# Tokens 512 to 767 of a product-key expert layer: all expert rows streamed through TensorE in place of gathered rows

## The reference, cut to what matters

```
q = (xt @ w_q).reshape(t, PEER_HEADS, 2, PEER_HALF)
s = einsum('thkc,knc->thkn', q, sub_keys)
top_s, top_i = top_k(s, 16)                    # per side, then 16 of the 256 sums
expert_idx, gate = ..., softmax(best_s)
h   = einsum('td,thkd->thk', xb, expert_u[ib])
act = gelu(h) * gb
out = einsum('thk,thkd->td', act, expert_v[ib])
h = layer_norm(DN_ALPHA * h + out)
```

## Time and profile before

| what | value |
|---|---|
| median of 3 runs | 3679.25 us (3676.4 to 3683.01) |
| profiled execution: span from first to last instruction | 3675.9 us |
| mean granted clock of PE | 0.852 |
| busy: PE, DVE, ACT, POOL | 78%, 73%, 28%, 56% of the span |
| moved by DMA | 1394.94 MB, 379 GB/s over the span |

### The profile page before, as it was taken

The page is one execution under the profiler, slowest core; times in us unless marked ns, Lnnn a source line. Parts: engine busy times, 40 slices in busy tenths (PEclk is TensorE's granted clock), DMA queues, the critical chain, the costliest instruction groups (busy, mean ns, idle before and its releaser), DMA issues.

```text
span 3675.9 us, 46161 instructions
## 1 busy us (share of the span) xinstructions
PE 2884.2 (78%) x16052; PEld 2038.9 (55%) x16052; DVE 2685.9 (73%) x5763; ACT 1040.2 (28%) x2694; POOL 2061.1 (56%) x1839
## 2 busy tenths in 40 slices
PE   8984988889889889999988869999977853443443
PEld 7884877578778436877775427878764410000000
DVE  3318874989874798778676887778776886667667
ACT  5511542234331213444412114444312110001000
POOL 0004543556554677777666676777656676555552
PEclk9997999899899889999999879999988866555555
DMA  6568998999888999999999999999999999999997
GB/s 245 211 226 317 395 410 355 399 376 358 323 336 332 411 410 402 393 406 409 388 411 411 410 393 410 408 400 393 410 392 407 396 405 413 421 421 421 421 420 313
DMA packets 316566, 1394.94 MB, mean 379 GB/s; under 512 B 35376, under 2 KB 40880, under 8 KB 251824
## 3 DMA queue, kind: packets, MB, share of 16 engines
q0 software_dynamic: 262656, 1073.86, 73.5%
q1 hardware_dynamic: 52384, 313.42, 21.5%
q10 hardware_dynamic: 1296, 4.72, 0.3%
HBM read 1387.66 MB, written 4.19 MB: 379 GB/s over the span
## 4 chain that ended last, share of the span: by engine, by line
PE 36%; DMA 27%; issue 14%; POOL 11%; DVE 9%; ACT 2%; DVEq 1%; SPq 0%; ACTq 0%; POOLq 0%
PE main L639 16%; DMA rowbuf<-ev,idx 9%; POOL rowbuf L596 8%; DMA rowbuf<-euv,idx 5%; PE main L647 4%; PE vbank L727 4%; PE main L838 3%; PE main L853 3%; DMA ring<-euv,idx 3%; DMA rowbuf<-eu,idx 2%; DVE rowbuf L1646 2%; DVE acc L1672 2%; PE turn L710 2%; DMA merged<-euv,idx 2%; DMA xT<-euv,idx 2%
## 5 line engine op out<-in xcount | busy, mean ns | idle before, releaser
L596 POOL DMA_INDIRECT rowbuf<-eu,idx x714 | 835.5, 1170 | 849.2 <-DVE hdot L1646 328.4
L596 POOL DMA_INDIRECT rowbuf<-ev,idx x713 | 767.3, 1076 | 370.6 <-issue 192.3
L1646 DVE CUSTOM_DVE_ANT_0 rowbuf<-rowbuf,hb 128x1024 f32<-128x1024 f32 x620 | 757.8, 1223 | 154.4 <-DMA rowbuf<-eu,idx 86.9
L639 PE MATMUL main<-xT,ring 128*128 128x256 f32 (+1 forms) x4480 | 804.6, 340 | 50.5 <-ACT mm L1109 39.8
L639 PEld LDWEIGHTS main<-xT,ring 128*128 128x128 f32 x4480 | 719.4, 193 | 138.5 <-issue 69.0
L727 PE MATMUL vbank<-rowbuf,vdiag 64*64 64x512 f32 x3008 | 512.3, 778 | 256.6 <-DMA rowbuf<-ev,idx 134.5
L1672 DVE SCALAR_TENSOR_TENSOR acc<-rowbuf,hact,acc 128x1024 f32<-128x1024 f32 x421 | 541.7, 1287 | 95.2 <-DMA rowbuf<-ev,idx 86.2
L727 PEld LDWEIGHTS vbank<-rowbuf,vdiag 64*64 64x64 f32 x3008 | 106.2, 158 | 581.2 <-ACT vdiag L1058 323.0
L1058 ACT ACTIVATE vdiag<-spots,hact 128x64 f32<-128x64 f32 x536 | 169.0, 343 | 553.6 <-DVE hact L1655 348.4
L838 PE MATMUL main<-late,ring 128*128 128x256 f32 (+1 forms) x1280 | 236.5, 348 | 36.7 <-issue 26.1
L1646 DVE CUSTOM_DVE_ANT_0 rowbuf<-rowbuf,hbank 128x1024 f32<-128x1024 f32 x178 | 215.8, 1216 | 47.1 <-DMA rowbuf<-eu,idx 39.1
(11 more groups left out here) (250 smaller groups left out, 3902.7 us busy)
## 6 DMA issues: line engine op xcount, KB each, us to landing
ring<-wblocks SPq DMA_DIRECT2D x280, 1024.0 KB, 8.2
rowbuf<-eu,idx POOLq DMA_INDIRECT x714, 12.6
rowbuf<-ev,idx POOLq DMA_INDIRECT x713, 13.1
pw<-poolw SPq DMA_DIRECT2D x20, 256.0 KB
h_out<-acc ACTq DMA_DIRECT2D x8, 512.0 KB, 7.5
xT<-xt SPq DMA_DIRECT2D x3, 1024.0 KB, 13.2
zy<-x SPq DMA_DIRECT2D x3, 1024.0 KB, 12.9
craw_ln<-ln1g SPq DMA_DIRECT2D x5, 512.0 KB, 14.5
```

The costliest lines, as they stand in the source:

```text
L596: pool.indirect_dma_start(rows[r], None, (eu, ev)[table], bass.IndirectOffsetOnAxis(ap=idx[c % 2][:, u, k:k + 1], axis=0)).then_inc(row_re ...
L639: last = pe.matmul(dst_[:, ct * tc:(ct + 1) * tc], w[:, k, ct * P:(ct + 1) * P], src[:, k, 0:tc], start=(k == 0), stop=(k == KD - 1))
L1646: last = dve.tensor_tensor_reduce(r, r, h, 1.0, 0.0, ALU.mult, ALU.add, hdot[:, g % 2, k:k + 1])
```

## The change: what it does

Superchunk 3 (`DENSE`, tokens 512 to 767, tiles 4 and 5) gathers no rows. Its picks leave the order of steps, which shrinks from 1024 to 768. In their place:

1. **Table of gates.** After the picks of superchunk 3 are known, they are split into row and column number of the 128 x 128 experts (`split_picks`) and transposed (`transposed_picks`). For each of the 256 tokens a product of two one-hot matrices (one with the gates as its values) gives a 128 x 128 matrix that holds the token's gate at each expert (`spread_gates`; `hot_rows` on DVE and `hot_columns` on ACT make the one-hot rows). 64 jobs of four tokens each do this at steps 489 to 531, around the end of superchunk 4's front; ACT evicts each job and stores the table in DRAM (`evict_job`, 16 stores of 1 MB).
2. **Experts.** 128 blocks of 1 MB (`dblocks`), each with U and V of 128 experts, come through the ring. PE scores a block for 256 tokens (`score_experts`), ACT takes the gelu (`gelu_experts`), DVE multiplies by a slice of the table (`weigh_experts`; slices for 8 blocks each are loaded by `load_slice` in pieces of 512 bytes), and PE adds the product with V into four banks (`sum_experts`, two blocks behind the score). The blocks are spread over steps 534 to 762.
3. **Around it.** `WIDTHS` gives superchunks 1 to 4 70, 140, 140 and 140 steps, so the front's last step is 513; `PAIRED` is 544. All convolutions are done on DVE (`FILL = NC`). There are 9 row buffers for 12, none of the ring's among the pair buffers (11 for 16), `LEAD2` is 4 for 7 and `GROUP` 2 for 4. Three sets of hidden rows, picks and gates are held for two (`HELD`). PE sums no row from step 534 on.

```diff
+DENSE = 3
...
-ROWS = 12
+ROWS = 9
...
-PAIRED = 800
-GROUP = 4
-LEAD2 = 7
+PAIRED = 544
+GROUP = 2
+LEAD2 = 4
-PAIRS = TILES * TILE
-WIDTHS = ((128, 28, 16, 42, 24), (40, 6, 6, 12, 12), (88, 16, 10, 34, 32), (124, 26, 16, 40, 38), (128, 28, 16, 42, 42))
+GATHERED = [t for t in range(TILES) if not FIRST[DENSE] <= t < FIRST[DENSE + 1]]
+GTILES = len(GATHERED)
+PAIRS = GTILES * TILE
+HELD = 3
+WIDTHS = ((128, 28, 16, 42, 24), (40, 8, 6, 8, 8), (81, 21, 12, 13, 13), (81, 21, 12, 13, 13), (81, 21, 12, 13, 13))
...
+FILL = NC
+
+
+SPREAD = 16
+QUAD = 4
+QUADS = NT * P // QUAD
+HOT = 4
+JOBS = 2 + QUADS + 4
+SPLIT_AT = BEGIN[NC - 1] + sum(WIDTHS[NC - 1][:2]) + 3
+JOB_BEGIN, JOB_END = BEGIN[NC - 1] + sum(WIDTHS[NC - 1][:3]) + 1, END + 18
+JOB_AT = [SPLIT_AT + 1] * 2 + [JOB_BEGIN + j * (JOB_END - JOB_BEGIN) // (JOBS - 2) for j in range(JOBS - 2)]
+DENSE_BEGIN, DENSE_END = JOB_END + 2, PAIRS - 6
+DENSE_AT = [DENSE_BEGIN + i * (DENSE_END - DENSE_BEGIN) // KEYS for i in range(KEYS)]
+SLICE = 8
+SLICES = KEYS // SLICE
+
+
...
+SHARES = ((0.0, 0.0, 0.0, 0.0), (0.2, 0.7, 1.0, 1.0), (0.1, 0.7, 1.0, 1.0), (0.1, 0.7, 1.0, 1.0), (0.1, 0.7, 1.0, 0.8))
...
+        both = [late[:, 0:2 * D], late[:, 2 * D:4 * D], early[:, :], merged[:, :, :].rearrange("p k t -> p (k t)"),
+                hb[(DENSE - 1) % HELD][:, :, :].rearrange("p t d -> p (t d)"), zy[:, :], mmscr[:, 0:2 * D]]
+        SPACES = len(both)
+        both += [rowbuf[:, r * D:(r + 2) * D] for r in range(0, ROWS - 1, 2)]
         BOTHS = len(both)
...
+            def load_slice(n):
+                sp.dma_start(slices[n % 2], spreadg[:, :, ds(n * SLICE * SPREAD, SLICE * SPREAD)].rearrange("g p n -> p g n")
+                             ).then_inc(slice_ready[n % 2], 16)
+
+            def load_expert(i):
+                r = i % RING
+                sp.wait_ge(block_done, NC * BLOCKS + i + 1)
+                sp.dma_start(ring[r][:, :, :], dblocks[ds(i, 1), :, :].rearrange("o p (k n) -> (o p) k n", k=KD)
+                             ).then_inc(w_ready[r], 16)
+
...
+            for i in range(RING):
+                load_expert(i)
+            for b in range(2):
+                sp.wait_ge(staged[b], 16 * SPREAD // 2)
+            for n in range(2):
+                load_slice(n)
+            for i in range(RING, KEYS):
+                load_expert(i)
+                n = i // SLICE + 1
+                if i % SLICE == 5 and 2 <= n < SLICES:
+                    sp.wait_ge(dense_weighed, (n - 1) * SLICE)
+                    load_slice(n)
...
+            def spread_gates(j):
+
+                g = j - 2
+                dst_ = job_bank(j)
+                pe.wait_ge(hot_row_ready, g + 1)
+                pe.wait_ge(hot_act_ready, g + 1)
+                for n in range(QUAD):
+                    last = pe.matmul(dst_[:, n * P:(n + 1) * P], hot_col[g % HOT][:, n, :], hot_row[g % HOT][:, n, :],
+                                     start=True, stop=True)
+                last.then_inc(job_made, 1)
+
+            def turned_hidden(j):
...
+            def score_experts(i):
+
+                if i == 0:
+                    pe.wait_ge(main_free, MAIN_AT[NC][0] + BANKS)
+                    pe.wait_ge(turn_free, TURN_AT[NC][0] + BANKS)
+                    pe.wait_ge(job_free, JOBS)
+                if i >= 2:
+                    pe.wait_ge(dense_gelu, i - 1)
+                pe.wait_ge(w_ready[i % RING], (NC * (BLOCKS // RING) + i // RING + 1) * 16)
+                w = ring[i % RING][:, 0:4, :].rearrange("p a (b n) -> p (a b) n", b=2)
+                dst_ = main[i % 2][:, 0:T]
+                for k in range(KD):
+                    last = pe.matmul(dst_, w[:, k, :], hTd[k // 4][:, k % 4, :], start=(k == 0), stop=(k == KD - 1))
+                last.then_inc(dense_scored, 1)
+
+            def sum_experts(i):
+
+                pe.wait_ge(dense_weighed, i + 1)
+                w = ring[i % RING][:, 4:8, :].rearrange("p a n -> p (a n)")
+                for n in range(NT):
+                    for half in range(2):
+                        last = pe.matmul(dsum[n][half], dact[i % 2][:, n * P:(n + 1) * P], w[:, half * 512:(half + 1) * 512],
+                                         start=(i == 0), stop=(i == KEYS - 1), skip_group_check=True)
+                last.then_inc(block_done, 1)
+
+            def experts(i):
+
+                score_experts(i)
+                if i >= 2:
+                    sum_experts(i - 2)
+                if i == KEYS - 1:
+                    sum_experts(i - 1)
+                    sum_experts(i)
+                    pe.wait_ge(block_done, NC * BLOCKS + RING + KEYS)
+                    pe.sem_inc(dense_done, 1)
+
+            at = now = 0
 
             def until(p):
...
+            def hot_columns(g):
+
+                if g == 0:
+                    act.wait_ge(pair_merged, NC * 4)
+                    act.wait_ge(job_free, 2)
+                if g >= HOT:
+                    act.wait_ge(job_made, 2 + g - HOT + 1)
+                for n in range(QUAD // 2):
+                    act.activation(hot_col[g % HOT][:, n, :], numbers[:, :], ACT.Square, scale=-1.0,
+                                   bias=colT[:, g * QUAD + n:g * QUAD + n + 1])
+                act.drain()
+                for n in range(QUAD // 2):
+                    t = slice(g * QUAD + n, g * QUAD + n + 1)
+                    last = act.activation(hot_col[g % HOT][:, n, :], hot_col[g % HOT][:, n, :], ACT.Relu, scale=minusT[:, t],
+                                          bias=gateT[:, t])
+                last.then_inc(hot_act_ready, 1)
+
+            def evict_job(j):
...
+            def evict_job(j):
+
+                act.wait_ge(job_made, j + 1)
+                src = hbank[:, (j % 2) * 512:(j % 2 + 1) * 512]
+                if j == 0:
+                    act.copy(rowT, src[:, 0:T])
+                    act.copy(colT, src[:, T:2 * T]).then_inc(job_free, 1)
+                elif j == 1:
+                    act.copy(gateT, src[:, 0:T])
+                    act.activation(minusT, src[:, 0:T], ACT.Copy, scale=-1.0).then_inc(job_free, 1)
+                elif j < 2 + QUADS:
+                    m, n = divmod(j - 2, SPREAD // QUAD)
+                    if n == 0:
+                        if m == 0:
+                            act.wait_ge(st_used, 2 * AJ * TILES + STATE)
+                        if m >= 2:
+                            act.wait_ge(staged[m % 2], 16 * (m // 2))
+                    to = staging[m % 2].rearrange("p (i t) -> p t i", t=SPREAD)[:, n * QUAD:(n + 1) * QUAD, :]
+                    act.copy(to, src.rearrange("p (t i) -> p t i", t=QUAD)).then_inc(job_free, 1)
+                    if n == SPREAD // QUAD - 1:
+                        act.wait_ge(job_free, j + 1)
+                        act.dma_start(spreadg[m, :, :], staging[m % 2]).then_inc(staged[m % 2], 16)
+                else:
+                    n, half = divmod(j - 2 - QUADS, 2)
+                    if n == 0:
+                        act.wait_ge(h_ready, TILES)
...
+            def gelu_experts(i):
+
+                act.wait_ge(dense_scored, i + 1)
+                if i >= 2:
+                    act.wait_ge(dense_weighed, i - 1)
+                act.activation(dgel[i % 2], main[i % 2][:, 0:T], ACT.Gelu
+                               ).then_inc(dense_gelu, 1)
...
+            def hot_rows(g):
+
+                if g == 0:
+                    dve.wait_ge(job_free, 2)
+                if g >= HOT:
+                    dve.wait_ge(job_made, 2 + g - HOT + 1)
+                t = slice(g * QUAD, (g + 1) * QUAD)
+                for n in range(QUAD // 2, QUAD):
+                    at_ = slice(g * QUAD + n, g * QUAD + n + 1)
+                    dve.tensor_scalar(hot_col[g % HOT][:, n, :], numbers[:, :], colT[:, at_], gateT[:, at_], ALU.is_equal, ALU.mult)
+                dve.tensor_tensor(hot_row[g % HOT], numbers[:, :].unsqueeze(1).to_broadcast([P, QUAD, KEYS]),
+                                  spread(rowT[:, t], KEYS), ALU.is_equal).then_inc(hot_row_ready, 1)
+
+            def weigh_experts(i):
+
+                n, m = divmod(i, SLICE)
+                dve.wait_ge(dense_gelu, i + 1)
+                if m == 0:
+                    dve.wait_ge(slice_ready[n % 2], 16 * (n // 2 + 1))
+                if i >= 2:
+                    dve.wait_ge(block_done, NC * BLOCKS + RING + i - 1)
+                dve.tensor_tensor(dact[i % 2].rearrange("p (g t) -> p g t", g=SPREAD),
+                                  dgel[i % 2].rearrange("p (g t) -> p g t", g=SPREAD),
+                                  slices[n % 2][:, :, m * SPREAD:(m + 1) * SPREAD], ALU.mult).then_inc(dense_weighed, 1)
+
+            def finish_dense(n):
+
```

More of the change, by code:

```diff
@@ L102, with at_step @@
 CONV = (0, 1, 3, 4)
-FILL = 3
+FILL = NC
[11 more added lines that the diff above has]
+SLICES = KEYS // SLICE
+def at_step(table, p):
+    return [n for n, q in enumerate(table) if q == p]
 def made_main(c, m):
@@ L196, in spans_of_bank @@
     found = []
```

(39 more changed lines are left out.)

271 lines of the change are left out of this document (162 added, 109 removed).

## The result

The changed kernel takes **3919.3 us** (median of 5 runs, 3916.23 to 3938.69) against 3679.25 us before: a ratio of 1.066, 95% interval 1.063 to 1.068. The sign of the forecast (3783 us, slower) was right, its size was not: 240 us were added where 104 had been forecast. The profiled execution has a span of 3937.0 us; it is the slowest of the five, 19 us above the execution that gives the median, so some 19 us of what follows belong to it alone.

The account below looks back on a forecast made before the run. Before, PE and DVE bound the front, with transfers close behind, and transfers alone the tail. Front 2688, tail 1072 and end 20 gave 3780 us, 3783 on the runs' scale, 2.8% slower; range 3570 to 3960.

Parts of the forecast that it names:

- front, to the first expert's score: Superchunks 1 to 4 and the table of gates, priced mainly by DVE's work: experts begin at 2688 us.
- PE's instructions, 128 experts: Tail: each expert block takes PE 7.07 us at full clock, 905 us for 128.
- start, and other stalls on DVE: Tail start: two slices must land before the first sum, 25 us (10 to 46).
- waits for blocks and slices: Tail: PE waits 72 us for late block landings and 70 us for blocks queued behind slices.
- clock and the rest: Tail: PE taken at full clock, 2.4 GHz, so nothing was added.
- after the last sum: End of kernel: evictions, norm and store, two dense tiles one behind the other, 20 us.
- The rival that dealt with it: Tail: stalls in each expert keep PE at 1.2 GHz, 905 us more, near 4690; chance 0.03.
- The ring: Tail: a block is freed only by its sum, leaving one expert's time for the next load; 72 us (0 to 322).
- the formula: Tail: with landing time L, each expert waits (L - 7.07)/2; 0.56 us taken, times 128.
- The slices' 70 us: Tail: fourteen 1 MB slices in 512-byte pieces delay the block behind them, 5 us each (0 to 238 in all).
- The slices' rival at 3951: Tail: slices served in turn with backlogged gathers land in 38 us, stalling 17 us each, 238 for 70; chance 0.19.
- The faster rival: PE sets the front, stage A 25 us shorter each; tail at transfers' pace, 966 us; 3602 us; chance 0.30.

Follow-up runs that it names:

- layout: Changed kernel with the gate table laid out by slices in DRAM, so a slice is read in 8 KB pieces: 3864.5 us.
- halves: Changed kernel with each expert block loaded as two 0.5 MB loads, U reloaded after its score, V after its sum: 3802.2 us, ratio 1.033.
- halves, slices on ACT: Changed kernel with each expert block loaded as two 0.5 MB loads and slices 2 to 15 issued on ACT's own queue: 3779.7 us.
- all three cures: Changed kernel with two 0.5 MB loads per block, slices on ACT's queue and the gate table laid out by slices: 3769.8 us, ratio 1.024.

## Why the prediction was right or wrong, step by step

| step | forecast | profile after | miss |
|---|---|---|---|
| front, to the first expert's score | 2688 | 2748 | +60 |
| PE's instructions, 128 experts | 905 | 128 x 6.88 = 881 | -24 |
| start, and other stalls on DVE | 25 | 10.5 + 25.3 = 36 | +11 |
| waits for blocks and slices | 72 + 70 = 142 | 164 | +22 |
| clock and the rest | 0 | 1156 - 881 - 36 - 164 = 75 | +75 |
| after the last sum | 20 | 3937 - 3904 = 33 | +13 |
| sum | 3780 | 3937 | +157 |

**The step that failed most was the clock.** It stood at nothing in the sum, and the 128 experts' instructions came 75 us dearer than their count at full clock. The rival that dealt with it was all or nothing: PE at half clock for the whole tail. I argued against it from stages in which PE was nearly always busy, and kept full clock. But one of those very rows had stage A at 0.94 with PE busy for 338 of 380 us, and I had worked out waits for each expert in the same paragraph. These come with a price of their own. By version, in profiled executions, from the first score to the last sum (us, waits with their number):

| version | tail | PE busy | above 881 | waits for blocks | waits for DVE |
|---|---|---|---|---|---|
| changed | 1156 | 956 | 75 | 164 (62) | 36 |
| no block loads | 922 | 886 | 5 | 0 | 35 |
| no slices | 1072 | 925 | 44 | 110 (79) | 37 |
| layout | 1081 | 921 | 40 | 126 (78) | 33 |
| halves | 1034 | 908 | 27 | 83 (9) | 42 |
| halves, slices on ACT | 1006 | 919 | 38 | 40 (110) | 45 |
| all three cures | 993 | 915 | 34 | 25 (17) | 45 |

So the 75 us lie inside PE's instructions and go with its waits. Counted from each instruction's start to the next one's, against 0.215 and 0.43 us, 58 of them fall in stretches that show half clock (181 of the 1156 us), and 17 in stretches at full clock, about 0.25 us for each of the 68 times that PE stops and starts. The version with halves and slices on ACT's queue has 7 us of the first kind and 31 of the second: its many short waits leave the clock alone and still cost something. Leaving out the slices took away 54 us of waits and 31 us inside the instructions, the layout 38 and 35; each won more than half as much again as the waits themselves.

**The ring was right in mechanism, a little low in size.** The landing was 8.0 us (forecast 8.2), so the formula gave 0.56 us for each expert, 72 us; without slices PE waited 110 us, with blocks landing in 8.8. The slices' 70 us are met by the 73 us of the run without them, but only if their clock is counted, which the forecast had at nothing. The slices' rival at 3951 and the forecast were one mechanism in two sizes. That the result of 3919 lies near the rival's is luck: slices cost 73 us and not its 238, and the rest came from the clock and the front.

**Small pieces and shared queues.** The Trainium skill ("DMA: Bandwidth & Descriptors", Specifications) gives 512 bytes as enough for line rate. Here, beside the gathers, a slice in such pieces took 17.2 to 19.4 us and one in 8 KB pieces 10.6 to 13.4, so in shared engines that size wasn't enough for the landing. The Trainium skill (same page, Queues, rings and completion order) says that an engine alternates between queues packet by packet. A slice of 512-byte pieces that lands in 58 to 63 us once a busy block queue runs beside its own, and in 10.6 us in 8 KB pieces, fits that.

**The front was 60 us late** in this execution, and 47 to 58 us in the six other versions with the same front, for four reasons that the trace shows in part. Superchunk 1 took 371 us for 353: fewer row buffers, which the prediction had at nothing, are worth 12 of these by their own run, and the rest is open. Superchunk 2 took 624 for 625. Superchunk 3 took 646, 21 more than its twin; its stage A had 395 us for 370, with a second norm of a tile (DVE waits 10.6 us for ACT there) in it, and why it cost that much isn't settled. Superchunk 4 needed 492 us to stage D for 476, and the jobs were dearer: one-hot rows of 128x128 took 0.34 us for the 0.25 that I assumed for one input, so DVE's part was 64 x 1.36 = 87 us for 77 (0.2 in the expectation of the run without jobs was a misreading of these rows), and ACT's eviction took 1.03 us for 0.58. These are the rows, mean ns behind the busy time:

```profile
L1855 DVE TENSOR_TENSOR zy<-numbers,BT 128x512 f32<-128x512 f32 x64 | 43.5, 679 | 0.0
...
L1854 DVE TENSOR_SCALAR lexp<-numbers,BT,CT 128x128 f32<-128x128 f32 x64 | 19.1, 340 | 2.4 <-PE hbank L817 2.4
...
L1217 ACT COPY state<-hbank 128x512 f32<-128x512 f32 x32 | 31.2, 1032 | 2.6 <-PE hbank L817 2.6
```

**A stall that I had the number for and didn't use.** Twenty-eight sums of V rows fall on one step (544), and I put them into the transfers and DVE's total only. DVE does them in a row, and the weighing of the next expert is queued behind them:

```profile
2799.87 13.17 DVE L1917 SCALAR_TENSOR_TENSOR acc<-rowbuf,hact,acc 128x1024 f32<-128x1024 f32 x10
...
2822.88 15.81 DVE L1917 SCALAR_TENSOR_TENSOR acc<-rowbuf,hact,acc 128x1024 f32<-128x1024 f32 x12 [1.85 <-DMA rowbuf<-ev,idx]
...
2843.09 0.42 DVE L1866 TENSOR_TENSOR lexp<-lexp,state 128x256 f32<-128x256 f32 x1
```

PE waited 25 us for that 0.42 us. DVE's load of 56% over the tail says nothing about it.

**The faster rival** needed the tail at 966 us and the experts' start at 2613. With all cures the tail was 993 us, but the start stayed at 2745 and the time at 3770, still behind. The cures' limit is the one that this rival named: transfers, at share 1.02 and 409 GB/s in the version with ACT's queue.

**The end.** After the last sum of an expert DVE still added gathered rows until 3929 us, which the forecast's 20 us did not have.

What remains open: 6 us of superchunk 1, the 21 of superchunk 3, the 16 of superchunk 4 before its stage D, and what sets the length of the stretch with the jobs.

## What to carry to other kernels

A transfer saved is worth time only where it was the limit, and work that replaces it costs what no stage hides: here 282 us were saved and 522 us added, because 881 us of PE and 145 MB went into a tail of gathers that lasted 610 us and had its transfers full. For streamed blocks, count how long a freed buffer has until it is needed again and compare that with the landing time under load; release what is read first as soon as it is read, and keep small-piece loads out of that queue. Price waits on PE at their length plus the slower instructions behind them: 75 us for 200 here.

## What the runs showed of the hardware that I had not expected

- A PE wait of 2 us was followed by eight 256-column instructions in 3.44 us for 1.89 (clock 0.92 over the tail, with 62 waits of up to 19.1 us); with 110 waits of at most 1.3 us the clock stayed 1.00.
- An ACT copy of 128x512 that writes every sixteenth element of its target took 1.03 us, a plain one 0.58.
- A DVE comparison and product with two per-partition scalars on 128x128 took 0.34 us, as much as an operation with two full inputs (0.35).
- PE's f32 instructions scale with their columns: from start to start eight of 256 columns took 1.73 us and four of 512 columns 1.71 to 1.73.
- Nine row buffers for twelve cost 89 us, 70 of them in the two superchunks where the transfers were full, though 4.5 steps of gathers had looked like enough cover.
